# A decoder trunk with two parallel branches: one gate projection moved from 8-product to 7-product matrix blocks, and part of a 31-tap convolution moved to ScalarE and DMA

## The reference

```python
hn = rms_norm(h, norm_g)                      # h: (528, 2048)
z  = hn @ w_in                                # (528, 7 * 2048)
xa, sa, vb, gb, sb, ma, mb = split(z)         # 2048 columns each
ya = rg_lru(causal_conv(xa, 4 taps), ...)     # two 128x128 gate matmuls per head, then a scan over tokens
ya = ya * silu(sa)
pa = ya @ w_proj_a
yb = causal_conv(vb * sigmoid(gb), 31 taps)
yb = silu(layer_norm(yb)) * silu(sb)
pb = yb @ w_proj_b
h  = h + (sigmoid(ma) * pa + sigmoid(mb) * pb) @ w_out
out = rms_norm(h, final_g)[16:]
```

## Time and profile before

| | us |
|---|---|
| median of three runs | 1796.1 (1795.7 to 1797.14) |
| the profiled execution | 1798.06 |
| its span, first to last instruction | 1796.5 |
| TensorE busy | 1772.9 (99%) |
| VectorE busy | 1290.4 (72%) |
| ScalarE busy | 719.7 (40%) |
| mean granted TensorE clock | 0.996 |

### The profile page before, as it was taken

How to read it: one execution, slowest core, us unless ns; L and a number is a source line. 1 busy time by engine, 2 the same in 40 slices (tenths; PEclk the granted TensorE clock), 3 DMA queues, 4 the chain that set the end, 5 groups by cost and what they waited for, 6 DMA issues and landing times.

```text
span 1796.5 us, 30396 instructions
## 1 busy us (share of the span) xinstructions
PE 1772.9 (99%) x12308; PEld 1662.0 (93%) x12308; DVE 1290.4 (72%) x1600; ACT 719.7 (40%) x960; POOL 178.8 (10%) x196
## 2 busy tenths in 40 slices
PE   9899999999999999999999999999999999999998
PEld 8799999999999999998999999999888899997886
DVE  7969797979888888889777766788623387663431
ACT  6543324242424242332555555555423154443322
POOL 0500000000000000000112111122100111111000
PEclk9999999999999999999999999999999999999999
DMA  6233333333333333344877756676667688848422
GB/s 205 64 107 95 112 93 107 101 107 94 110 93 105 100 93 111 93 135 135 223 223 201 220 155 180 158 203 182 235 216 234 175 215 199 194 132 269 153 82 94
DMA packets 217127, 269.68 MB, mean 150 GB/s; under 512 B 7504, under 2 KB 187856, under 8 KB 215888
## 3 DMA queue, kind: packets, MB, share of 16 engines
q1 hardware_dynamic: 168240, 188.21, 32.6%
q0 software_dynamic: 48800, 80.23, 18.2%
HBM read 227.52 MB, written 40.89 MB: 149 GB/s over the span
## 4 chain that ended last, share of the span: by engine, by line
PE 93%; DVE 3%; issue 2%; DMA 1%; ACT 1%; POOL 0%; SPq 0%; DVEq 0%; ACTq 0%; POOLq 0%
PE psum L687 52%; PE psum L724 30%; PE psum L879 6%; PE psum L893 2%; PE psum L784 1%; DMA t_lo<-m_spill 1%; DMA raw<-in_w_proj_a 1%; DVE region L1733 0%; DMA region<-in_x_channels 0%; DVE region L1370 0%; DVE t_lo L1652 0%; DVE w_lo L1294 0%; DVE total L1420 0%; DVE c_lo L1385 0%; POOL t_lo L603 0%
## 5 line engine op out<-in xcount | busy, mean ns | idle before, releaser
L687 PE MATMUL psum<-x_hi,w_hi 128*128 128x264 f32 (+1 forms) x1888 | 452.8, 306 | 7.5 <-ACT w_hi L908 3.0
L687 PE MATMUL psum<-x_lo,w_hi 128*128 128x264 f32 (+1 forms) x1888 | 452.4, 306 | 0.0
L687 PEld LDWEIGHTS psum<-x_hi,w_hi 128*128 128x128 f32 x1888 | 306.7, 189 | 23.2 <-ACT w_hi L908 3.5
L1316 DVE SCALAR_TENSOR_TENSOR region<-region,conv_cols 128x512 f32<-128x512 f32 x480 | 326.8, 747 | 0.0
L687 PEld LDWEIGHTS psum<-x_lo,w_hi 128*128 128x128 f32 x1888 | 306.4, 189 | 14.9 <-issue 0.2
L908 ACT ACTIVATE w_hi<-raw 128x1024 fp32r<-128x1024 f32 x128 | 135.6, 1059 | 437.4 <-PE psum L687 399.5
L687 PE MATMUL psum<-x_hi,w_lo 128*128 128x264 f32 (+1 forms) x1888 | 290.9, 304 | 0.0
L687 PEld LDWEIGHTS psum<-x_hi,w_lo 128*128 128x128 f32 x1888 | 260.2, 188 | 14.9
L1294 DVE TENSOR_TENSOR w_lo<-raw,w_hi 128x1024 fp32r<-128x1024 f32 x128 | 158.2, 1236 | 59.8 <-ACT w_hi L908 59.7
L1536 DVE TENSOR_TENSOR w_lo<-region,w_hi 128x1024 fp32r<-128x1024 f32 x87 | 106.5, 1224 | 85.5 <-ACT w_hi L1079 85.3
L1536 DVE TENSOR_TENSOR x_lo<-region,x_hi 128x1024 fp32r<-128x1024 f32 x87 | 106.3, 1223 | 69.4 <-ACT x_hi L1079 67.9
(11 more groups left out here) (226 smaller groups left out, 3206.8 us busy)
## 6 DMA issues: line engine op xcount, KB each, us to landing
raw<-in_w_in SPq DMA_DIRECT2D x140, 512.0 KB, 3.5
region<-in_w_in SPq DMA_DIRECT2D x42, 1024.0 KB, 6.5
region<-in_w_proj_b SPq DMA_DIRECT2D x16, 1024.0 KB, 7.5
raw<-in_w_out SPq DMA_DIRECT2D x32, 512.0 KB, 4.0
raw<-in_w_proj_a SPq DMA_DIRECT2D x31, 512.0 KB, 3.5
region<-in_w_in POOLq DMA_DIRECT2D x21, 512.0 KB, 6.4
sigmoid_spill<-wide POOLq DMA_DIRECT2D x16, 512.0 KB, 5.3
aux<-conv_b_spill POOLq DMA_DIRECT2D x16, 512.0 KB, 5.7
```

The costliest lines, as they stand in the source:

```text
L687: last = pe.matmul(psum[:, bank, 0:width], weights[:, s, k, m * P:(m + 1) * P], operand[part][:, place(4 * group + k), t0:t0 + width], sta ...
L1316: ins = dve.scalar_tensor_tensor(conv_b[:, t, :], moved, w, conv_b[:, t, :], ALU.mult, ALU.add)
```

## The change

1. **sa leaves the bodies.** In the first body its four chunks become the first ma item (`first_ma`), gated and spilled at once. In bodies 1 to 7 they are gone (`ITEMS_BODY = 12`). sa is computed in eight units between those of mb and sb, so there are 28 units ahead of the w_proj_a product (`STD = 4`, `NX = 4 * PAIRS - STD`), still three plain items, now with other banks. The scan's result h is spilled in the body (`spill_h`), loaded again (`load_h`) and multiplied with silu(sa) behind each sa unit (`gate_ya`), and ya is spilled from there.
2. **Bodies 1 to 7 by tile.** A chunk is now one tile of 128 columns by eight row blocks, so each tile takes two chunks: xa 0, xa 1, gb 0, gb 1, vb 0, vb 1, on bank pairs 0, 2, 4, 0, 2, 4. It has 48 matmuls of 264 columns as before. The gate rounds stand ahead of chunks 4 to 7. Loops are unrolled, and the copies of parameter columns are gone.
3. **Eight of 31 taps of conv_b** are made elsewhere in bodies 1 to 7: ScalarE writes the first tap (with the bias) to `conv_by_act`, then seven products; each product is added by an accumulating DMA from POOL's queue, two tiles in turn, each add waiting for the one before on its tile. VectorE joins the two sums at the end (`join_conv`). The first tap of conv_a is ScalarE's too. The sums into `total` for the mean are accumulating DMAs (`sum_conv`) but for the last pair.

In the diff the three functions `branch_body` are those of TensorE, ScalarE and VectorE, in this order.

```diff
-BODY = 16
+BODY, ITEMS_BODY = 16, 12
...
-        STD = 3
-        NX = 3 * PAIRS - STD
+        STD = 4
+        NX = 4 * PAIRS - STD
...
-        MA, MB, SB, PA, PB = range(5)
+        MA, MB, SA, SB, PA, PB = range(6)
+        ACT_TAPS = 8
+        STEPS_AT = {1: (0,), 2: (1,), 3: (2, 3), 4: (4,), 5: (5,), 6: (6,)}
...
+                for p in range(ITEMS_BODY):
+                    n, half = item_chunk(i, p), p % 2
+                    column = (COL_XA, COL_GB, COL_VB)[p // 4] + 256 * i + P * (p // 2 % 2)
+                    sp.wait_ge(lo_ready, n + 1 - RING)
+                    sp.dma_start(raw[:, n % RING, :].rearrange("p (k n) -> p k n", n=P),
+                                 w_in_v[:, KH * half:KH * (half + 1), column:column + P])
...
+            def sum_conv(i):
+                for j in (2 * i - 2, 2 * i - 1):
+                    wait(pool, conv_summed, 16 * j)
+                    pool.dma_start(total[:, :], conv_b[:, j % 2, :], accum_op=ALU.add).then_inc(conv_summed, 16)
...
+            def add_taps(i, s):
+                n = (ACT_TAPS - 1) * (i - 1) + s
+                for t in range(2):
+                    if s == 0:
+                        pool.wait_ge(conv_begun, 2 * i - 1 + t)
+                    wait(pool, tap_added[t], 16 * n)
+                    pool.wait_ge(tap_ready[t], n + 1)
+                    pool.dma_start(conv_by_act[:, t, :], products_at(s + 1, t), accum_op=ALU.add)
+                        .then_inc(tap_added[t], 16)
...
+            for i in range(1, PAIRS):
+                load_gates(i)
+                spill_h(i - 1)
+                if i > 1:
+                    spill_conv(i - 1)
+                    sum_conv(i - 1)
+                for step in range(ACT_TAPS - 1):
+                    add_taps(i, step)
...
+            def branch_body(i):
+                for p in range(ITEMS_BODY):
+                    if p == 0:
+                        pe.wait_ge(gb_sigmoid, 2 * i)
+                    elif p == 2:
+                        pe.wait_ge(vb_gated, 2 * i - 1)
+                    elif p == 4:
+                        pe.wait_ge(vb_gated, 2 * i)
+                        pe.wait_ge(gate_hi_ready, i + 1)
+                        pe.wait_ge(gate_lo_ready, i + 1)
...
+                    if 4 <= p < 8:
+                        gate_round(i, p - 4)
+                    item(i, p)
...
+            def tap_product(i, s):
+                n, k = (ACT_TAPS - 1) * (i - 1) + s, s + 1
+                for t in range(2):
+                    j = 2 * i - 2 + t
+                    if s == 0:
+                        act.wait_ge(h_ready, 2 * i)
+                    elif s == 1:
+                        act.wait_ge(vb_gated, 2 * i)
+                    else:
+                        act.wait_ge(tap_added[t], 16 * (n - 1))
+                    act.activation(products_at(k, t), yb_pad[:, t, META + k:META + k + SEQ], ACT.Copy,
+                                   scale=params[:, j, CONV_B_W + k:CONV_B_W + k + 1]).then_inc(tap_ready[t], 1)
...
             def branch_body(i):
+                for p in range(ITEMS_BODY):
+                    chunk_hi(item_chunk(i, p))
+                    if p == 1:
+                        t_hi_of(i - 1)
+                        first_tap(i)
                     if p == 2:
+                        xa_copy(i, 0)
                     if p == 3:
                         cut_gates_hi(i)
+                    if p == 4:
+                        cut_c_hi(i, 0)
+                        xa_copy(i, 1)
+                    for step in STEPS_AT.get(p, ()):
+                        tap_product(i, step)
+                    if 5 <= p < 9:
+                        read_gates(i, p - 5)
+                    if 5 <= p < 8:
+                        cut_c_hi(i, p - 4)
...
-            TAPS = [0, 3, 3, 3, 3, 1, 1, 3, 2, 3, 2, 3, 3, 1, 0, 0]
+            TAPS = [0, 3, 3, 1, 2, 1, 3, 3, 3, 2, 2, 0]
...
             def branch_body(i):
+                for p in range(ITEMS_BODY):
+                    chunk_lo(item_chunk(i, p))
                     if p == 0:
+                        t_sums(i - 1)
+                    if p == 3:
+                        t_lo_of(i - 1)
+                        conv_a_taps(i, range(1, KA), (0,), conv)
                     if p == 4:
                         cut_gates_lo(i)
+                    if p == 5:
+                        conv_a_taps(i, range(1, KA), (1,), conv)
+                    if 4 <= p < 8:
+                        cut_c_lo(i, p - 4)
+                    if p == 9:
+                        gated = gate_inputs(i)
                     if p == 10:
+                        factor = scale_inputs(i, gated)
+                    conv_b_taps(i, p, taps, ACT_TAPS)
+                    if p == 11:
+                        scan(factor)
+                        join_conv(i, taps)
+                        gate_vb(i, 0)
+                gate_vb(i, 1)
```

More of the change, by code:

```diff
@@ L48 @@
 CONV_A_W = 8
-PER_BRANCH_BODY = 80
 WARM_UP = 18
@@ L364, in spills @@
         def spills(w):
-            return sum(32 if n // PAIRS == SB else 16 for n in range(w % 2, w, 2))
+            return sum(32 if n // PAIRS == SB else 16 for n in range(w % 2, w, 2) if n)
+        PLAIN_BANKS = {1: 6, 2: 0, 3: 3}
         PA_BANKS = (0, 6, 2, 4)
@@ new lines, in first_body, with item, passes @@
+                pe.wait_ge(gates_read, 4)
+                for g in range(4):
+                    multiply(0, 12 + g, all_tokens(((4, 5), (6, 7))), g)
+            def item(i, p):
+                n, half, bank = item_chunk(i, p), p % 2, 2 * (p // 2 % 3)
+                hi, lo = (w[:, n % RING, :].rearrange("p (k n) -> p k n", n=P) for w in (w_hi, w_lo))
+                def passes(weights, parts):
+                    for k in range(KH):
+                        for part in parts:
+                            for h in range(2):
+                                last = pe.matmul(
+                                    psum[:, bank + h, 0:HALF], weights[:, k, :],
+                                    part[:, KH * half + k, h * HALF:(h + 1) * HALF],
+                                    start=half == 0 and k == 0 and weights is hi and part is x_hi,
+                                    stop=half == 1 and k == KH - 1 and weights is lo)
+                    return last
+                pe.wait_ge(hi_ready, n + 1)
+                passes(hi, (x_hi, x_lo))
+                pe.wait_ge(lo_ready, n + 1)
+                passes(lo, (x_hi,)).then_inc(multiplied, 1)
@@ L1214, in _ @@
             first_body()
-            with act.Fori(1, PAIRS) as i:
-                steps.at(2 * i)
+            for i in range(1, PAIRS):
                 branch_body(i)
@@ L1317, in conv_b_taps @@
                                                            ALU.mult, ALU.add)
-                        if k == KB - 1:
+                        if k == KB - 1 and not first:
                             ins.then_inc(conv_b_done, 1)
@@ L1321, in conv_b_taps, with join_conv @@
                             before[t] = steps(ins)
+            def join_conv(i, before):
+                for t in range(2):
+                    dve.wait_ge(tap_added[t], 16 * (ACT_TAPS - 1) * i)
+                    steps.done(before[t])
+                    dve.tensor_tensor(conv_b[:, t, :], conv_b[:, t, :], conv_by_act[:, t, :], ALU.add)\
+                        .then_inc(conv_b_done, 1)
             def add_total(i):
                 for t in range(2):
[L1326 to L1327 removed]
+                    dve.wait_ge(conv_b_done, 2 * i - 1 + t)
+                    dve.wait_ge(conv_summed, 32 * (i - 1))
+                    wait(dve, summed, t)
                     dve.tensor_tensor(total[:, :], total[:, :], conv_b[:, t, :], ALU.add).then_inc(summed, 1)
@@ L1792, in _ @@
             first_body()
-            start = steps.total()
-            with dve.Fori(1, PAIRS) as i:
-                steps.at(plus(i * PER_BRANCH_BODY, start - PER_BRANCH_BODY))
+            for i in range(1, PAIRS):
                 branch_body(i)
-                assert steps.n == PER_BRANCH_BODY, steps.n
-            steps.at(start + (PAIRS - 1) * PER_BRANCH_BODY)
             TAPS[:] = [2, 3, 3, 3, 3, 3, 3, 3, 3, 3, 2, 0]
```

474 lines of the change are left out of this document (253 added, 221 removed).

## The result

The changed kernel takes 1804.8 us (median of 7, 1801.6 to 1808.4) against 1796.1 us (median of 7, 1794.9 to 1799.2), a ratio of 1.0047 with the 95% interval 1.0037 to 1.0058. Forecast was 1787.8 us, faster. The time lies in the stated range, the sign is wrong. The profiled execution has a span of 1802.8 us.

The account below looks back on a forecast made before the run. Both stages were taken as bound by TensorE's matmul issue pace. Units save 15.3 us and stalls of 1.0 us in seven bodies cost 7.0, so 1796.1 - 8.3 = 1787.8 us; range 1781 to 1809.

Parts of the forecast that it names:

- What TensorE gains: Seven sa items of 22.12 us leave bodies 1 to 7, seven units of 19.93 us come instead: 15.3 us less.
- The walk along VectorE: VectorE's work followed through a body: c_lo 0 0.1 to 0.2 us late, c_lo 1 0.8; 1.0 us stall per body.
- I take L = 4.4 us: Landing time of one 256 KB accumulating DMA into the taps' sum, put at 4.4 us.
- the other tile's transfer 0.7 us ahead or behind: In the taps' additions, the two tiles' accumulating DMAs were taken to run 0.7 us apart.
- 3L: Three dependent additions on a tile before product 5; c_lo 1 comes at 16.8 + 3L, 30.0 us with L = 4.4.
- the 5.1 at which the change stops paying: Addition landing time L giving 2.19 us stall per body, c_lo 1 at 32.2; from there on slower than before.
- rival (b): The accumulation chain decides: L = 6.1, 5.0 us stall per body, 1816 us; chance 0.28.
- rival (c): TensorE's gain goes into stalls of 1.7 to 2.7 us per body: 1793 to 1799.7 us, no change; chance 0.18.
- The interpolation: For a 256 KB addition: half the 2.8 us surcharge of a 512 KB accumulation, on a plain store's 2.7, gives 4.1.
- The chunk loads in 512 B rows: Weight loads in bodies, rows of 512 B instead of 1 KB: hidden whether landing in 3.5 or 6.4 us.
- The second place: At body start, two dependent accumulations into total land at 4.1 us, before VectorE's first tap at 5.6; late from L = 5.1.

Follow-up runs that it names:

- with the stalls gone the kernel: Changed kernel with ScalarE's and VectorE's orders changed, a pair of taps moved from slot 3 to slot 2, and six taps elsewhere instead of eight: 1781.4 us.
- the two kernels that take the additions out of the way: Changed kernel with ScalarE's products behind gate reads and c_hi, products 3 to 6 one slot later: 1789.6 us; changed kernel with half of each tap addition: 1788.4 us.
- the first kernel: Changed kernel with ScalarE's products behind gate reads and c_hi, and products 3 to 6 one slot later: 1789.6 us.
- The run with half of ScalarE's order: Changed kernel with ScalarE's products behind gate reads and c_hi, but product 3 still in slot 3 ahead of hi 4: 1791.3 us.
- VectorE's order after ScalarE's: Changed kernel with ScalarE's products later, c_lo 1 ahead of conv_a's taps of tile 1, and one pair of taps from slot 2 to slot 4: 1786.2 us.

## Why the prediction was wrong

**What TensorE gains** was right. Units stayed at 19.93 us, and with the stalls gone the kernel is at 1781.4 where 1796.1 - 15.3 = 1780.8. That this fits to 0.6 us is partly luck: the instructions of a body cost 72.96 us, 0.3 less than forecast, which alone is 2.2 us in seven bodies that the medians don't show.

**The walk along VectorE** was right in its places and its moments. It gave 1.0 us of stall on 73.27, a body of 74.3, and this body was measured at 74.30 and 74.31 in the two kernels that take the additions out of the way. That both agree to 0.1 us is luck: on the 72.96 us without a stall, the stall is 1.3 us, and two errors of 0.3 cancel. The walk split the stall as 0.15 and 0.8 us; the first kernel shows 0.43 and 0.45 us of idle time ahead of the two rounds.

**The step that failed is "I take L = 4.4 us"** with "the other tile's transfer 0.7 us ahead or behind". The median landing was 4.9 us, three in a row took 5.0 us each on tile 1, and tile 1 ran 1.3 us behind. c_lo 1 came at 32.4 instead of 30.0. (The terms behind 3L add up to 16.7, not 16.8, which changes nothing.) By the forecast's own formula L was above 4.7, where the chain takes over, and at an L of 5.2, c_lo 1 at 16.8 + 15.6 = 32.4, past the 5.1 at which the change stops paying. The mechanism is rival (b)'s, which had a chance of 0.28; its size is nearer to rival (c), since L is 5 and not 6.1, and the time lies between the two. Halving the transfer and reordering ScalarE each showed that it was this term. The interpolation took half of 2.8 us as what an accumulation adds to a plain 256 KB store; the measured 4.9 is 2.2 above the 2.7 of that store. So the surcharge didn't halve with the bytes. Its base was mixed, too: the m_spill row holds eight plain and eight accumulating stores, and the plain ones landed in 4.5 us at the median there, not in the 3.3 of conv_b's spill. Why an addition takes 4.9 us is not settled; the overlap with the chunk loads goes along with it.

**A place was missed.** The forecast followed the additions only to product 5 and c_hi 1. Product 3 stood ahead of hi 4 in the same way, and in the body shown ScalarE waited 2.4 us there and TensorE 1.0 us for c_lo 0, where VectorE's order alone leaves 0.43. The run with half of ScalarE's order shows that this place adds next to nothing to the body there, since the later wait shrinks by what the earlier one took. In the changed kernel the same holds by argument: the chain to c_lo 1 begins at product 1, ahead of both waits.

**The sum, with measured sizes.** -15.3 for seven units; seven bodies of 75.90 instead of 73.27, +18.4; together +3.1. By the chains of both profiles the way from body 1 to the first unit, with 139.5 us for the seven added units, is 4.6 us longer than before, which holds also body 1's longer first wait. The span grew by 6.3 us and the median by 8.7. The kernel reaches body 1 1.3 us earlier, and the rest of the span's growth is 3.0 us after the start of the w_proj_a product, where both kernels run the same instructions; that stretch takes 504.0 to 508.3 us in the twelve profiles of this study (505.3 before, 508.3 after, the ten experiments 504.0 to 507.5), so no cause in the change is shown for it. The median moved 2.4 us more than the two profiled spans mainly because the profiled execution of the kernel before, at 1798.06 us, was itself 2.0 us above its median.

**The rest of the forecast.** The chunk loads in 512 B rows were hidden at 4.2 us to landing. VectorE's work in a body was 62.6 us (forecast 62), ScalarE's 40.4 (forecast 44). The second place, the sums into total at the body's start, was in time but for one wait of 0.77 us, as the forecast had it; it showed only once the other stalls were gone. The load of h, the spill of ya and VectorE's multiplication in the sa units cost nothing. TensorE didn't wait at the plain items for anything new.

## What to carry to other kernels

On an engine that runs its program in order, place an instruction that waits for a DMA behind everything in its slot that the bounding engine needs, and ask of each such wait what is queued behind it, not only who reads its result. A chain of n dependent transfers multiplies the error of one transfer's price by n: here an error of 0.6 us, tripled, made the sign of the change, so a forecast with such a chain should name the price at which it breaks even, and the order of work should be made so that it doesn't matter. When two paths end close together, shortening one shows nothing until the other is gone (3.4 us for VectorE's order after ScalarE's, nothing before). And when the long stalls are gone, look at the single bodies: the sums into total then cost 77.7 us instead of 72.96 in one body of six.

## What the runs showed of the hardware

An accumulating DMA from SBUF to SBUF of 256 KB (128 rows of 2 KB) lands in 4.9 us at the median and in 3.2 to 6.3 us, beside weight loads of 512 KB per 5.8 us; one of 128 KB lands in 3.4. In the one chain followed here, of three on tile 1 beside those on tile 0, they ran at 5.0 us each. A plain 256 KB store had landed in 2.7 us. The Trainium skill (DMA: Bandwidth & Descriptors, Anatomy of one DMA) gives 2.0 us plus the bytes at 436 GB/s, an estimate of 2.6 and 2.3 us for the two sizes; the 1.5 us between the two sizes here (with rows of 2 KB and of 1 KB) is five times the 0.3 us of that rate, and the measurement decides.

A chunk of 48 matmuls without a gate round took 5.83 us in the unrolled body, against 5.87 in the loop.
